# Layer norms of a hybrid encoder: VectorE adds the last two feature groups and their squares, TensorE sums the one addend

## The reference, cut to what matters

```python
def layer_norm(x, g, b):
    xf = x.astype(jnp.float32)
    mu = jnp.mean(xf, -1, keepdims=True)
    var = jnp.mean(jnp.square(xf - mu), -1, keepdims=True)
    return ((xf - mu) * lax.rsqrt(var + EPS) * g + b).astype(x.dtype)

x = layer_norm(ALPHA * x + 0.5 * swiglu(x, lw['w_ffn1_in'], lw['w_ffn1_out']), g[0], b[0])
x = layer_norm(ALPHA * x + mix, g[1], b[1])
x = layer_norm(ALPHA * x + memory_attend(x, mem_k, mem_v, lw['mem_w_q'], lw['mem_w_o']), g[2], b[2])
x = layer_norm(ALPHA * x + 0.5 * swiglu(x, lw['w_ffn2_in'], lw['w_ffn2_out']), g[3], b[3])
```

## Time and profile before

| what | value |
|---|---|
| median of 3 runs | 2773.28 us |
| the profiled execution: time / its span | 2772.52 us / 2770.7 us |
| TensorE busy | 2741.7 us (99%) |
| VectorE busy | 1800.5 us (65%) |
| ScalarE busy | 1160.6 us (42%) |
| GpSimd busy | 543.2 us (20%) |
| mean granted TensorE clock | 0.998 |

### The profile page before, as it was taken

One profiled execution on the slowest core, in us unless ns is written; L12 is line 12 of the kernel. 1 busy time (PEld: TensorE's weight loads), 2 busy tenths in 40 slices (PEclk: granted clock), 3 DMA queues, 4 the chain that ended last, 5 costly groups with the idle time before them and its releaser, 6 DMA issues.

```text
span 2770.7 us, 53831 instructions
## 1 busy us (share of the span) xinstructions
PE 2741.7 (99%) x21690; PEld 2647.3 (96%) x21690; DVE 1800.5 (65%) x2826; ACT 1160.6 (42%) x1800; POOL 543.2 (20%) x227
## 2 busy tenths in 40 slices
PE   8999999999999999999999999999999999999998
PEld 8999999799999899999999999987999998999997
DVE  6777665655436478777587776666554274777775
ACT  4343354522335353433454334544223353634343
POOL 0000133134372220000300001331443722100002
PEclk9999999999999999999999999999999999999999
DMA  4333322132362123333323332221323621233322
GB/s 158 104 93 92 100 86 87 31 92 87 93 213 76 46 82 94 93 99 92 92 88 99 92 99 92 82 84 40 90 88 100 206 69 54 80 97 92 93 99 71
DMA packets 75771, 257.95 MB, mean 93 GB/s; under 512 B 10704, under 2 KB 15696, under 8 KB 74256
## 3 DMA queue, kind: packets, MB, share of 16 engines
q1 hardware_dynamic: 68432, 240.66, 28.4%
q10 hardware_dynamic: 7104, 13.94, 1.4%
HBM read 246.70 MB, written 7.87 MB: 92 GB/s over the span
## 4 chain that ended last, share of the span: by engine, by line
PE 92%; DVE 3%; DVEq 2%; issue 1%; ACT 1%; DMA 0%; ACTq 0%; PEldq 0%
PE PS L487 91%; DVEq L1823 1%; DVE Y L1743 1%; PE PS L886 1%; ACT LNT L1246 0%; DVE O L1746 0%; PE PS L1184 0%; DVE XL L1743 0%; DVE LNT L1746 0%; DVEq L2215 0%; DVE P L2223 0%; DVE LNT L1784 0%; DVEq L2423 0%; DMA WR<-in_w 0%; ACTq L1540 0%
## 5 line engine op out<-in xcount | busy, mean ns | idle before, releaser
L477 POOL TENSOR_TENSOR WL<-WR,WH 128x1024 fp32r<-128x1024 f32 x223 | 543.0, 2447 | 2185.4 <-ACT WH L1246 2185.4
L487 PE MATMUL PS<-XH,WH 128*128 128x272 f32 x2464 | 598.1, 292 | 10.2 <-DVE XL L1743 9.6
L487 PE MATMUL PS<-XL,WH 128*128 128x272 f32 x2464 | 587.8, 289 | 0.0
L1246 ACT ACTIVATE WH<-WR 128x1024 fp32r<-128x1024 f32 x450 | 464.6, 1052 | 199.4 <-DMA WR<-in_w 169.2
L487 PEld LDWEIGHTS PS<-XH,WH 128*128 128x128 f32 x2464 | 425.2, 188 | 19.3 <-issue 9.8
L487 PEld LDWEIGHTS PS<-XL,WH 128*128 128x128 f32 x2464 | 426.2, 189 | 0.8 <-issue 0.5
L487 PE MATMUL PS<-XH,WL 128*128 128x272 f32 x2464 | 426.5, 288 | 0.0
L1246 ACT ACTIVATE LNT<-PS 128x272 f32<-128x272 f32 (+4 forms) x318 | 142.7, 454 | 568.3 <-PE PS L487 553.2
L487 PEld LDWEIGHTS PS<-XH,WL 128*128 128x128 f32 x2464 | 354.1, 188 | 0.4
L487 PE MATMUL PS<-HH,WH 128*128 128x272 f32 x1408 | 298.5, 289 | 0.0
L487 PE MATMUL PS<-HL,WH 128*128 128x272 f32 x1408 | 297.4, 288 | 0.0
(11 more groups left out here) (273 smaller groups left out, 5047.7 us busy)
## 6 DMA issues: line engine op xcount, KB each, us to landing
WR<-in_w SPq DMA_DIRECT2D x450, 512.0 KB, 3.7
MRAW<-in_mem ACTq DMA_DIRECT2D x2, 1024.0 KB, 5.0
MKs<-in_memk_in ACTq DMA_DIRECT2D x2, 1024.0 KB, 6.2
MVs<-in_memv_in ACTq DMA_DIRECT2D x2, 1024.0 KB, 9.9
out_mem_k<-MKp ACTq DMA_DIRECT2D x2, 1024.0 KB, 6.4
out_mem_v<-MVp ACTq DMA_DIRECT2D x2, 1024.0 KB, 8.6
out_y<-Y SPq DMA_DIRECT2D x3, 544.0 KB, 3.0
Y<-in_x ACTq DMA_DIRECT2D x2, 544.0 KB, 7.0
```

The lines of the kernel that those rows point to most:

```text
L477: pool.tensor_tensor(WL[s][:, :], WR[s][:, :], WH[s][:, :].bitcast(F32), ALU.subtract).then_inc(lo_ready[s], 1)
L487: return pe.matmul(out, lhsT, rhs, start=start, stop=stop, skip_group_check=True)
L1246: return act.activation(out, in_, func, **kw)
```

## The change

In both halves of the tokens, and in all 8 norms, VectorE adds the last two groups of Y into a new tile Y67 (`pair_sum`, behind a drain) and the two squares into SQ[0] (`pair_sq`, behind the wait on ScalarE's squares). `norm_last` has two products with ones instead of four, behind waits on the new semaphores pair_sum and pair_sq. Y67 lies on the last group of XL, which is free at that time. In half 0 both additions stand between `residual_last(0)` and `head(0)`; in half 1 pair_sum follows `residual_last(1)` at step 2 and pair_sq closes step 3. To make room for two semaphores, the three for the stores of krope, ckv and pool become one (st_small), and each of their waits now waits for all seven stores of the layer.

```diff
+        XL0 = at[0]
         XL = place("XL", KC * T + PAD, F32R)
+        Y67 = nc.alloc_sbuf_tensor_at("Y67", [128, T], F32, offset=XL0 + 7 * T * 4)
...
             def norm_last(l, i, h):
 
-                for g, m in enumerate(SPLIT[i]):
-                    pe.wait_ge(S["y_last"], split(l, i, h, g))
-                    r = mm(PS[:, 4 + h, 0:TH], ONES, Yf[:, ch(m, h)], False, m == KC - 1)
-                r.then_inc(S["st_s"], 1)
-                for g, m in enumerate(SPLIT[i]):
-                    pe.wait_ge(S["sq_last"], split(l, i, h, g))
-                    r = mm(PS[:, 6 + h, 0:TH], ONES, SQ[m % 2][:, hs(h)], False, m == KC - 1)
-                r.then_inc(S["st_q"], 1)
+                pe.wait_ge(S["pair_sum"], 2 * (4 * l + i) + h + 1)
+                mm(PS[:, 4 + h, 0:TH], ONES, Y67[:, hs(h)], False, True).then_inc(S["st_s"], 1)
+                pe.wait_ge(S["pair_sq"], 2 * (4 * l + i) + h + 1)
+                mm(PS[:, 6 + h, 0:TH], ONES, SQ[0][:, hs(h)], False, True).then_inc(S["st_q"], 1)
...
+                def pair_sum(h):
+                    ve.drain()
+                    tt(Y67[:, hs(h)], Yf[:, ch(6, h)], Yf[:, ch(7, h)], ALU.add).then_inc(S["pair_sum"], 1)
+
+                def pair_sq(h):
+                    ve.wait_ge(S["sq_last"], split(l, i, h, 1))
+                    settle(ve)
+                    tt(SQ[0][:, hs(h)], SQ[0][:, hs(h)], SQ[1][:, hs(h)], ALU.add).then_inc(S["pair_sq"], 1)
...
                 residual_last(0)
+                pair_sum(0)
+                pair_sq(0)
                 head(0)
...
                     if g == 2:
                         residual_last(1)
+                        pair_sum(1)
+                    if g == 3:
+                        pair_sq(1)
...
-                ve.wait_ge(S["st_ck"], (l + 1) * 32)
+                ve.wait_ge(S["st_small"], (l + 1) * 112)
```

## The result

The changed kernel has a median of 2777.52 us (2776.56 to 2779.65, 22 runs), the kernel before on the same chip 2773.38 us (2772.4 to 2775.03, 22 runs). The ratio is 1.0015 [1.0009, 1.0022]: 4.1 us, 0.15%, slower. The forecast was +5.4 us.

A forecast was written before the change was run, and what follows sets the result against it. Each norm was taken as bound by TensorE until half 0's sum, then VectorE from the mean to XL of group 6. Half 1 +6.2, half 0 -0.9, N7 +0.1 gave +5.4 us: 2778.6 us, range 2774.8 to 2783.0.

The forecast's parts named there:

- The bound: Each norm: TensorE until half 0's sum, then VectorE from mean to XL of group 6; TensorE, though busy, waits there.
- Half 0: N0 to N6: one product less on the chain (0.455 us), partly lost because GpSimd holds pair_sum(0); sum -0.90 us.
- Half 1: Mean to TensorE's restart: pair_sum(1) and pair_sq(1) make VectorE's XL 0.88 us later per norm, 7 x 0.88 = 6.2 us.
- The strict reading: Half 1: every operation waits for the pipe to empty, so pair_sq costs 0.52 instead of 0.355, 1.2 us more over seven norms.
- What the lead covers: Before group 6 TensorE arrives about 1 us ahead of XL and stays the waiting engine; norm_last(1) still ends earlier than before.
- N7: Last norm, no next phase: step 3 starts 0.25 us early, pair_sq(1) takes 0.355 of it; +0.1 us.
- The stores: VectorE's rotary key copy also waits for pool stores, which land 4.3 us before it; no cost.
- The records: Trace records of products with ones: 32 on Y67 instead of 64 on Y.
- TensorE as the bound: Rival 1: TensorE bounds the kernel, so its 14.6 us come off: 2758.7 us; chance 0.08.
- pair_sum(0) not held: Rival 2: GpSimd doesn't hold half 0's addition, giving 7 x -0.455 = -3.2 us: 2776.3; chance 0.12.
- XL of group 3 losing the lock: Rival 3, half 1: GpSimd's subtraction goes first and XL of group 3 waits; 0.54 us per norm, 2782.4; chance 0.12.
- The sum: Whole program: half 1 +6.2, half 0 -0.9, N7 +0.1, together +5.4 us.

The follow-up runs named there:

- TensorE's part alone: Kernel before with two products with ones instead of four per half, no VectorE additions, group 6 left out of the sums: 2768.92 us, ratio 0.9984.
- their own run: Kernel before with only the three store semaphores merged into one: 2773.19 us, ratio 1.0001.
- the squares of half 1 alone: Kernel before with only the addition of the two squares in half 1, Y keeping its two products: 2775.86 us, ratio 1.0010.

## Why the prediction was right, step by step

**The bound.** Right. The term that was to decide the sign is that TensorE's busy time doesn't bound the norms; TensorE's part alone gave 4.6 us of 14.6.

**Half 0.** Right in mechanism, off by 0.3 us in size: -1.21 instead of -0.90. pair_sum(0) was held in all of N0 to N6 and not in N7, where GpSimd does nothing; the mean moved by -0.23 in N0 (predicted -0.25) and +0.04 in N1 (+0.10). The other norms gave -0.23, -0.09, -0.25, -0.23 and -0.22 where -0.10, -0.20, -0.14, -0.15 and -0.16 were forecast. The mis-sized term is the distance in time between the last new Y and GpSimd's end, which I took from the trace of before for each norm. It wasn't kept: in N2 GpSimd ended 1.34 us after that Y's start before, and 1.20 after it now; in N3 the shift went the other way. The rule of the Trainium skill that spoke against the change, in "SBUF — State Buffer", section "Who interferes with whom", held: one operand from PSUM freed the instruction (two in 0.79 us beside GpSimd's 2.55), and without GpSimd's step VectorE's queue had no stall.

**Half 1.** Right: 0.88 per norm in N0, N1, N2, N4 and N6 to within 0.04 (0.92, 0.87, 0.89, 0.87, 0.88). In the changed kernel GpSimd was first, as worked out, and both parts have their size: 0.53 for the drained addition, 0.36 for the undrained. The strict reading of the Trainium skill, "VectorE: DVE Perf Modes", section "The DRAIN you can't avoid" (0.52 for pair_sq), doesn't fit this measurement of 0.36. The sum is 5.73 and not 6.2 because two norms of the kernel before contained a stall of 0.35 and 0.14 us (mean to restart 17.89 in N3, 17.68 in N5) that isn't there in the changed kernel. I had multiplied the usual norm by seven and had not looked at how even the seven were before. One reading in the walk is slightly off: it took GpSimd's 2.40 us in the earlier trace rows as its time alone, and in half 1 of the changed kernel, where VectorE doesn't hold it, that is 2.37. It moves nothing in the sum.

**What the lead covers.** Before group 6 TensorE waits 1.03 us by the prediction's own count (0.88 of idle time), where about 1 was forecast. It idles for 1.07 before group 2 and only 0.19 before group 3. Right where it decides.

**N7.** +0.12, as forecast (+0.1): 0.46 gained ahead of the mean, 0.58 lost behind it. **The stores.** Nothing, as forecast; shown by their own run. **The records.** 32 on the addend instead of 64 on Y, though the profile calls it Y and not Y67.

**The rivals.** TensorE as the bound: excluded by the run of TensorE's part alone. pair_sum(0) not held: excluded by 0.96 to 1.24 us in seven norms. XL of group 3 losing the lock: it did not happen in any norm of the changed kernel, since GpSimd asks 0.32 after XL of group 3 starts (387.38, 387.70), as worked out; I made no run that forces it, so its price of 0.54 per norm is untested.

**The sum.** +5.4 was forecast. The profiled executions differ by 4.85, the medians by 4.1; the terms that were off are half 0 (0.3) and the stalls of before (0.5), and 0.2 came from between the norms. The other 0.7 us between the profiled executions and the medians is scatter of single executions: the 22 runs of the changed kernel span 3.1 us.

Two things stay open. The one-off stalls of 0.13 to 0.37 us in the mean to restart stand in other norms in other kernels (N3 and N5, N0 and N3, N6), in four kernels one of about 0.34 stands in N7, and the trace names nothing that they wait for. And the start of the program up to the last new Y of N0 takes between 374.84 us (the changed kernel) and 376.43 us (the squares of half 1 alone) in the one profiled execution of each, though the norms' code hasn't run before it. I didn't try to settle either.

## What to carry to other kernels

Before work is moved from a busy engine to a less busy one, find in the chain, in order of time, who waits for whom at the end of the stretch: here the engine that was 99% busy was waiting in each norm for the one that was 65% busy. Look at what runs beside the new place: VectorE's additions of two SBUF tiles should stand clear of GpSimd's work, or take one operand from PSUM, and it can pay to do a step of 1.22 us on VectorE rather than have 2.4 us of it on GpSimd hold VectorE. And an addition costs by what stands before and behind it: 0.36 us in the flow, 0.53 between two drains.

## What the runs showed of the hardware

- A held VectorE operation of 128x272 ended 0.30 to 0.31 us after GpSimd's end in every norm of the changed kernel and of the kernel before, and GpSimd's own 2.37 us grew where VectorE was at the lock first: to 2.40, 2.49, 2.56 and 2.67 in half 0 of the changed kernel where it began 0.14, 0.22, 0.30 and 0.41 before the end of VectorE's addition into SUMS (N6, N5, N4, N1).
- VectorE makes the low part of a 128x1024 chunk in 1.22 us. GpSimd took 2.34 us at the least, 2.40 in the median, and up to 2.68 around the norms, where VectorE held it.
- A VectorE addition or multiplication of 128x272 with one operand from PSUM took its usual 0.42 to 0.44 us inside a subtraction of GpSimd, as `tt` and as `stt`.
- Behind a wait, TensorE's product with ones started 0.05 to 0.06 us after VectorE's event, not 0.16 as I had reckoned; the extra 0.11 shows as a longer first matmul (0.39 to 0.40 instead of 0.29).
- A kernel in which TensorE is 99% busy got 0.15% slower when 32 of its products were replaced by additions on VectorE, and 0.31% faster when 16 were replaced so that no addition was held, one product of each norm was moved ahead, and VectorE took a step over from GpSimd.
